# A distance table added to attention scores: on the vector engine with the row maxima, in place of a product with the identity

## What is computed

```python
DIL_PATTERNS = ((128, 1), (512, 4), (2048, 16))
def dilated_window_attention(q, k, v, rel_bias, window, dilation):
    ...
    bias = jnp.transpose(rel_bias[t5_bucket(rel * dilation)], (2, 0, 1)).astype(jnp.float32)
    logits = jnp.einsum('brnqhd,brnkhd->brnhqk', qs, kw).astype(jnp.float32) * (dh ** -0.5) + bias
    logits = jnp.where(mask[:, None], logits, -jnp.inf)
    m = jnp.max(logits, axis=-1, keepdims=True)
    e = jnp.exp(logits - m)
    den = jnp.sum(e, axis=-1, keepdims=True)
    o = jnp.einsum('brnhqk,brnkhd->brnqhd', (e / den).astype(v.dtype), vw)
    lse = (m + jnp.log(den))[..., 0]
    ...
```

## Time and profile before

| | |
|---|---|
| median of 3 runs | 3674.65 us |
| the runs | 3672.95 to 3678.0 us |
| profiled execution, first to last instruction (no other time of it is given) | span 3676.4 us |
| TensorE busy | 3588.7 us, 98% |
| vector engine busy | 1833.9 us, 50% |
| ScalarE busy | 1525.4 us, 41% |
| GpSimd busy | 1151.8 us, 31% |
| L1418, the product with the identity | 144 of 17929 matmuls |
| L1617 and L1620, the maxima in attention | 480 and 60 reductions, 688 and 419 ns each |

### The profile page before, as it was taken

One profiled execution on the slowest core, in us unless ns is written; L12 is line 12 of the kernel. 1 busy time (PEld: TensorE's weight loads), 2 busy tenths in 40 slices (PEclk: granted clock), 3 DMA queues, 4 the chain that ended last, 5 costly groups with the idle time before them and its releaser, 6 DMA issues. The chain is left out here.

```text
span 3676.4 us, 49277 instructions
## 1 busy us (share of the span) xinstructions
PE 3588.7 (98%) x17929; PEld 2974.7 (81%) x17929; DVE 1833.9 (50%) x2860; ACT 1525.4 (41%) x2535; POOL 1151.8 (31%) x841
## 2 busy tenths in 40 slices
PE   8999999999999999999999999999999999999998
PEld 7788777778788888888767877777778888888886
DVE  4134868946434334344551367799453334443335
ACT  4344878965212212211342367788552212211223
POOL 1143543434322221221342334534343212211213
PEclk9999999999999999999999999999999999999999
DMA  5442221123111111111324423211221111111113
GB/s 174 124 114 69 76 62 36 27 81 104 35 46 39 35 40 34 40 40 34 114 68 137 121 53 81 53 40 27 92 81 52 38 37 34 41 39 34 39 41 115
DMA packets 235043, 234.11 MB, mean 64 GB/s; under 512 B 42188, under 2 KB 196126, under 8 KB 234847
## 3 DMA queue, kind: packets, MB, share of 16 engines
q1 hardware_dynamic: 234887, 232.09, 21.6%
HBM read 173.86 MB, written 51.48 MB: 61 GB/s over the span
## 5 line engine op out<-in xcount | busy, mean ns | idle before, releaser
L241 PE MATMUL ps<-hh,wh 128*128 128x512 f32 (+1 forms) x2544 | 917.0, 360 | 18.2 <-PEq L235 14.3
L242 PE MATMUL ps<-hl,wh 128*128 128x512 f32 (+1 forms) x2544 | 904.1, 355 | 0.0
L243 PE MATMUL ps<-hh,wl 128*128 128x512 f32 (+1 forms) x2544 | 903.1, 355 | 0.0
L2575 POOL TENSOR_TENSOR wl<-raw,wh 128x1024 fp32r<-128x1024 f32 x126 | 301.8, 2402 | 1268.0 <-ACT wh L2408 1268.0
L2636 DVE SCALAR_TENSOR_TENSOR cb<-ps,params,cb 128x1023 f32<-128x1023 f32 (+1 forms) x172 | 143.9, 878 | 871.3 <-ACT cb L2417 871.3
L241 PEld LDWEIGHTS ps<-hh,wh 128*128 128x128 f32 x2544 | 483.3, 190 | 92.7 <-issue 20.8
L242 PEld LDWEIGHTS ps<-hl,wh 128*128 128x128 f32 x2544 | 483.4, 190 | 72.4 <-issue 5.7
L243 PEld LDWEIGHTS ps<-hh,wl 128*128 128x128 f32 x2544 | 482.7, 190 | 68.1
L1656 DVE TENSOR_TENSOR pl<-ps,ph 128x512 fp32r<-128x512 f32 (+1 forms) x576 | 375.4, 652 | 66.1 <-ACT ps L1498 65.7
L1384 PE MATMUL ps<-q,k 97*128 97x512 f32 (+4 forms) x1296 | 385.6, 388 | 13.1 <-DVE pl L1656 6.1
L1497 ACT ACTIVATE ph<-ps 128x512 fp32r<-128x512 f32 (+1 forms) x576 | 329.9, 573 | 157.5 <-PE ps L1384 152.7
(11 more groups left out here) (284 smaller groups left out, 5776.5 us busy)
## 6 DMA issues: line engine op xcount, KB each, us to landing
raw<-in_w_up SPq DMA_DIRECT2D x88, 512.0 KB, 3.9
raw<-in_w_down SPq DMA_DIRECT2D x44, 512.0 KB, 3.6
heads<-stage SPq DMA_DIRECT2D x28, 640.0 KB, 3.4
rq<-heads SPq DMA_DIRECT2D x56, 320.0 KB, 4.0
raw<-in_w_in SPq DMA_DIRECT2D x32, 512.0 KB, 4.4
rk<-heads SPq DMA_DIRECT2D x32, 320.0 KB, 4.6
raw<-in_w_out SPq DMA_DIRECT2D x16, 512.0 KB, 4.1
residual<-my SPq DMA_DIRECT2D x32, 256.0 KB, 2.0
```

The lines of the kernel that those rows point to most:

```text
L241: pe.matmul(out, wh, xh, start=(k == 0), stop=False)
L242: pe.matmul(out, wh, xl, start=False, stop=False)
L243: last = pe.matmul(out, wl, xh, start=False, stop=(k == len(pairs) - 1))
L2575: pool.tensor_tensor(c.wl[slot][:], c.raw[parity][:], c.wh[slot][:].bitcast(F32), ALU.subtract).then_inc(w_lo, units)
```

## The change

In kind B the product with the identity goes, and TensorE no longer waits for `table_hi` before a maximum's tile. The vector engine waits for it instead, and one call adds the table's stretch to the scores and takes the row's maximum. For tiles 8 and 9, whose result is wanted with its sign turned, the call scales by -1 and takes the minimum. The sum is written back to the same PSUM bank.

```diff
 max_scores, TensorE
-                    if kind(h) == "B":
-                        pe.wait_ge(table_hi, 2 * (h - 3))
                     r = 96 if kind(h) == "A" else P
...
-                    mm = pe.matmul(out, c.q1[h % 3][0:r, qt * P:qt * P + P], keys, start=True, stop=kind(h) != "B")
-                    if kind(h) == "B":
-                        x0 = 1024 + qt * P - k0 - w
-                        mm = pe.matmul(out, c.ident_r[:], c.gh[h % 2][:, x0:x0 + w], start=False, stop=True)
-                    mm.then_inc(max_scored, 1)
+                    pe.matmul(out, c.q1[h % 3][0:r, qt * P:qt * P + P], keys, start=True, stop=True).then_inc(max_scored, 1)
...
 take_max, vector engine
                     dve.wait_ge(max_scored, NM * h + j + 1)
-                    if qt < 8:
+                    if kind(h) == "B":
+                        dve.wait_ge(table_hi, 2 * (h - 3))
+                        x0 = 1024 + qt * P - k0 - w
+                        table = c.gh[h % 2][:, x0:x0 + w].bitcast(F32)
+                        if qt < 8:
+                            dve.tensor_tensor_reduce(out=bank(c, b, w), in0=bank(c, b, w), in1=table, scale=1.0, scalar=-3.0e38,
+                                                     op0=ALU.add, op1=ALU.max, accum_out=c.mx[:, qt, kb:kb + 1]).then_inc(max_taken, 1)
+                        else:
+                            m0 = max_column(qt)
+                            dve.tensor_tensor_reduce(out=bank(c, b, w), in0=bank(c, b, w), in1=table, scale=-1.0, scalar=3.0e38,
+                                                     op0=ALU.add, op1=ALU.min, accum_out=c.m[:, m0:m0 + 1]).then_inc(max_taken, 1)
+                    elif qt < 8:
                         dve.tensor_reduce(c.mx[:, qt, kb:kb + 1], bank(c, b, w), AX.X, ALU.max).then_inc(max_taken, 1)
```

## The result

| | before | after |
|---|---|---|
| median of 4 runs each, same chip | 3674.97 us | 3653.01 us |
| the runs | 3672.95 to 3678.0 | 3648.9 to 3653.27 |
| profiled span | 3676.4 | 3651.5 |

The ratio is 0.9936, 95% interval 0.9922 to 0.995: 22.0 us less, with an interval of 18 to 29. The forecast was 27.8 us less and 3647. The two profiled spans lie 24.9 us apart. A span is some 2 us shorter than the time of the same execution (after: 3651.5 for 3653.27), so the execution profiled after lies at its median and the one before, by estimate, some 3.5 us above its own. Of the 24.9, 24.3 us are in the two stretches of attention (453.2 + 454.6 us before, 440.9 + 442.6 after, from the first exponential to the last). All that follows is told from the profiled executions, by head.

The account below looks back on a forecast made before the run. TensorE was taken to bound heads 4 to 6. Per layer, head 3's 2.15, heads 4 to 6's 10.4 and head 7's 1.38 make 13.9 us; both layers 27.8, from median 3674.65 to 3647 us, range 3641 to 3660.

Parts of the forecast that it names:

- The bound: In heads 4 to 6 TensorE has no room (head 5: busy 36.06 of 36.2 us); every other engine has nine microseconds.
- the rival that its rows hide waits: Products were free: another engine's chain paces the attention step and the time remains 3674 us; chance 0.07.
- The chain of the third row: Steps 7 to 9 of a B head: fixed 4.23 us, so products of steps 7 and 8 gain nothing in heads 4 to 6.
- Head 3: Head 3 of each layer: 0.90 + 1.85 - 0.6 = 2.15 us gained.
- The first part: Head 3, steps 6 to 8: table wait and three products together gain 0.90 us, limited by ScalarE's row copy.
- The second part: Head 3, steps 9 to 17: products give 1.85 us, less 0.6 for lateness behind the split of values.
- Heads 4 to 6: Each of these heads gains 14 x 0.23 + 2 x 0.12 = 3.46 us; three heads 10.4 a layer.
- The vector engine's price: Each biased maximum, now two instructions, costs the vector engine 0.16 us more, between 0 and 0.345; covered by TensorE.
- the high end: Dearest case for a biased maximum on the vector engine: 0.345 us more; head 5 then busy 31.4 of 32.7 us.
- At most 2.2 us: Cost of high-end maxima behind the split of values: 0.23 x 3 heads + 0.4 in head 3, two layers.
- The pace of the vector engine: Rival: a maximum costs about 0.45 us more, the vector engine sets the pace part-time; gain 15, 3660 us; chance 0.10.
- the half rate: Rival: the vector engine's sum runs at half rate, a maximum 0.68 us more; 12.8 us slower, 3687; chance 0.05.

Follow-up runs that it names:

- experiment 3: Changed kernel with the third row of maxima of B heads turned at step 6, not 7: 3647.86 us, ratio 0.9923.
- experiment 8: Kernel before, identity product in place, with the third row of B heads turned at step 6: 3671.72 us against 3676.23, ratio 0.9989.
- experiment 2: Changed kernel with a plain maximum, the table left out of the maxima: 3652.52 us, ratio 0.9939.
- experiment 4: Changed kernel with the split of the next head's values in two, cast at step 9 and remainder at step 10: 3648.64 us, ratio 0.9932.
- experiment 11: Changed kernel with third row at step 6, values split at steps 9 and 10, row of ones on GpSimd at step 8: 3643.09 us, ratio 0.9907.
- experiment 5: Changed kernel with an extra unread 256-column reduction of the table ahead of each biased maximum: 3658.94 us, ratio 0.9954.
- experiment 6: Changed kernel with an extra unread table reduction, as many columns as the maximum, ahead of each biased maximum: 3677.37 us, ratio 1.0004.
- experiment 9: Changed kernel with third row at step 6 and values split at steps 13 and 14: 3690.62 us against 3676.89, ratio 1.0035.

## Right and wrong, step by step

**The bound.** Right. TensorE had no room in heads 4 to 6, and the rival that its rows hide waits (3674) fell: with the row's chain out of the way, 3.81 of the 3.92 us of products came back in head 5 (experiments 3 and 8).

**The chain of the third row.** Right, and the main term. It took 4.30 us in head 5 and 4.22 to 4.26 in the others, where 4.23 was forecast; the idle time shown at step 9 of heads 4 to 6 is 0.55 to 0.66 where 0.6 to 0.8 was; moving the row gave 6.3 us of attention.

**Head 3.** The first part came out exactly: steps 6 to 9 in the kernel after are

```profile
418.95 0.87 PE L1384 MATMUL ps<-q,k 97*128 97x512 f32 x3
...
422.69 0.25 ACT L1472 ACTIVATE row_part<-ps 4x128 fp32r<-4x128 f32 x1
...
424.78 0.94 PE L1384 MATMUL ps<-q,k 97*128 97x512 f32 x3 [0.33 <-DMA q<-row_part]
```

From copy to use are 2.09 us, and the scores of steps 6 to 9 now span 5.83 us where they spanned 6.73 (420.74 to 427.47, the second in the earlier trace rows): 0.90 less. The second part failed: **"with two dearer maxima in that chain I take off 0.6"**. The stall behind the split of values is there, but the maxima aren't dearer, a plain one leaves the head as long (experiment 2), and the size is wrong: of the 1.85 us of products in steps 9 to 17, 0.99 came back in layer 1 and 0.76 in layer 2, so the stall cost 0.86 and 1.09. These rows of head 3, steps 11 to 13, show why:

```profile
428.32 1.29 POOL L1528 TENSOR_TENSOR q<-rq,q 64x512 fp32r<-64x512 f32 x1
...
428.83 1.13 DVE L619 CAST vh<-vt 128x640 fp32r<-128x640 f32 x1
...
429.72 0.86 PE L1384 MATMUL ps<-q,k 97*128 97x512 f32 x3
...
430.00 0.90 DVE L621 TENSOR_TENSOR vl<-vt,vh 128x640 fp32r<-128x640 f32 x1
...
432.16 0.62 PE L1384 MATMUL ps<-q,k 97*128 97x256 f32 x3 [0.64 <-DVE pl L1661]
```

The step from 429.72 to 432.16 takes 2.44 us where its neighbours take 1.62: 0.82 lost. The cast takes 1.13 us where it takes 0.48 when left alone. In the kernel before head 3's cast took 485 ns; the products' going moved it into a GpSimd row. Experiment 4 gave 0.28 us of this back. The 0.34 that was borrowed from head 2 was too small besides, as this is the same place in the kernel before:

```profile
399.16 0.86 PE L1384 MATMUL ps<-q,k 97*128 97x512 f32 x3
...
399.87 0.94 DVE L619 CAST vh<-vt 128x640 fp32r<-128x640 f32 x1
...
400.78 0.86 PE L1384 MATMUL ps<-q,k 97*128 97x512 f32 x3
```

With the scores at 402.92 that step takes 2.14 us where the one before takes 1.62, so 0.34 us of idle time shown were 0.52 lost, and there too the cast was slow. The further 0.23 us of layer 2 lie at steps 14 and 15 and stay unexplained.

**Heads 4 to 6.** 3.46 us each was forecast, 3.0 to 3.2 came. Head 4 lost 0.3 to the vector engine's row of ones (experiment 11), which had been hidden behind nine products a step and isn't behind eight; I hadn't listed it at all. Behind the split of values 0.07 to 0.17 a head went (experiment 4), and the chain's 4.30 for 4.23 took 0.07 of head 5. The prediction had 0.12 us of room behind the split with dear maxima, and at the measured price it would have been 0.40. What used it up is the split itself, which the prediction took to be as long as in the kernel before. There cast and remainder took 0.48 and 0.83 us in heads 4 to 6; now one of them meets a GpSimd row in each of these heads, and the two are 0.34 to 0.42 us longer together. In head 5:

```profile
494.29 0.48 DVE L619 CAST vh<-vt 128x640 fp32r<-128x640 f32 x1
494.33 1.04 POOL L1528 TENSOR_TENSOR q<-rq,q 64x256 fp32r<-64x256 f32 x1
...
494.81 1.24 DVE L621 TENSOR_TENSOR vl<-vt,vh 128x640 fp32r<-128x640 f32 x1
```

With the row moved, in experiment 3, the two took 0.57 and 0.91 us in head 5 and TensorE didn't wait behind them.

**The vector engine's price.** Too high: 0.16 us a maximum, measured 0.02, since the accumulator's read runs beside the next instruction. It changed nothing in the sum (experiment 2). But the cost that I gave the high end was too low. "At most 2.2 us" at 0.345 a maximum, said the prediction (its own sum, 0.90 - 0.46 - 2 x 0.345, leaves minus 0.25 and not minus 0.23, so 2.3); at 0.34, experiment 5 measured 7.2 us of attention, 4.7 of it in heads 3 and 4, where the vector engine has the split and the row of ones as well. A mean of 31.4 busy of 32.7 hid that some steps had no room.

**The rivals.** The pace of the vector engine and the half rate both hang on the price, and at 0.02 neither arose. The half rate's point of decision, 0.6 us a maximum, came out in the sum (experiment 6: 907.6 of 907.8 us at 0.60), partly by luck, since head 5 won 0.9 there and head 4 lost as much. And the row that spoke for a half rate was misread: the mean of 2623 ns hides two kinds of L1166 in the kernel before.

```profile
202.12 2.39 POOL L679 TENSOR_TENSOR wl<-raw,wh 128x1024 fp32r<-128x1024 f32 x1 [10.24 <-ACT wh L674]
202.96 2.90 DVE L1166 TENSOR_TENSOR stage<-rot,pr 128x1280 f32<-128x1280 f32 x1 [6.29 <-ACT pr L1051]
...
264.66 1.49 DVE L1166 TENSOR_TENSOR stage<-rot,pr 128x1280 f32<-128x1280 f32 x1
```

Eight of the ten ran beside GpSimd rows and took 2.90 to 2.92 us; the two with GpSimd idle took 1.49, as L1160 does. That is the delay of the last section and no rate of the engine. The rule of the Trainium skill that the prediction weighed (Vector Engine (DVE) Microarchitecture Reference, section 7) is about two SBUF sources, and the sum has one beside one in PSUM; with an accumulator it ran at 696 ns for 512 columns, where the reduction takes 688, so the rule doesn't reach this form.

## What to carry to other kernels

When an engine is relieved, every wait of fixed length that its work used to cover comes out: list them (a DMA's round trip, a split between two low parts, a write of constants) and give each the slack that is left, step by step and not as a mean over the head. Lengths of vector rows beside GpSimd are no constants: look at what GpSimd runs when they will start. Then move what starts such a chain in the same edit: here one step earlier for the row and one step apart for the split took the gain from 22 us to 33. Before moving work on one engine, follow who waits for the buffer that it frees, through each queue, SP's too.

## What the hardware showed

**The accumulator's read is free.** Its row of 137 ns starts together with the instruction behind it, and sum to low part takes 0.62 us where reduction to low part took 0.60.

**A cast on the vector engine waits for GpSimd's running instruction.** L619, a copy of 640 float32 columns within SBUF, takes 0.48 us alone. In the rows of head 3 above GpSimd's subtraction ends at 428.32 + 1.29 = 429.61, and the cast, begun at 428.83, ends at 429.96: 0.35 us later. Of the 20 casts in the kernel after, nine began 0.2 us or more before the end of a GpSimd row that was already running, L1528 each time; they finished 0.350 to 0.354 us after its end, whatever they took (553 to 1130 ns). The other eleven took 481 to 484. The Trainium skill (SBUF — State Buffer, section "Who interferes with whom") says that casts on the vector engine can take the port pair which that engine shares with GpSimd, and that whoever issues first has it for the whole instruction while the other blocks; the trace agrees. So such a cast isn't priced by its mean of 642 ns but by what GpSimd has running when it starts, and a change that moves TensorE by half a microsecond can add 0.65 us to it.

**The remainder is slowed as well.** L621, a subtraction with both sources in SBUF, takes 0.83 us when GpSimd is idle beside it; in the kernel after it took 0.90 to 1.24 wherever a GpSimd row ran beside it, and in experiment 9 up to 1.67. In head 3 GpSimd met the cast in experiment 4 (1.14 and 0.81 us) and the remainder in experiment 11 (0.48 and 1.45); the sums are the same, and TensorE's idle time at step 14 is 0.36 and 0.34.
